# Three rounded score products in place of one full-precision product, the next heads earlier in a pair, and the start and end of a gated mixer in another order

## The reference, cut to what matters

```
# first block, layer l = 0, 1; x is 512 x 1024, ctx is 256 x 1024
h = modulate(rms_norm(x, g_mix[l]), sh1, sc1)          # the same for ctx
f_in, c_q, c_kv, k_rope = split_in_proj(h @ w_in[l])
q = (rms_norm(c_q, g_q) @ w_q_b).reshape(b, n, 12, 96)  # 64 plain + 32 rotated
k, v = from c_kv and k_rope                             # 64 plain + 32 rotated shared
s = einsum(q_nope, k_nope) + einsum(q_rope, k_rope)     # 768 keys
att = softmax(s * 96 ** -0.5) @ v
x = x + gt1 * (concat(fourier_mix(f_in), att) @ w_out[l])
x = x + gt2 * conv_ffn(modulate(rms_norm(x, g_ffn[l]), sh2, sc2))
# layer 0 does the same for ctx, whose 256 queries see the 256 context keys

# second block, the first mixer; hn is the normed output of the first block
proj = hn @ w_in
q, k, v = silu(causal_conv(proj_a)); q, k = l2norm(q), l2norm(k)
oa = rmsnorm(gated_delta_rule(q, k, v, g, beta), norm_a) * silu(z)
ob = rmsnorm(mlstm_chunkwise(qb, kb, vb, i_log, f_log), norm_b) * o_gate
mixed = concat(oa, ob) @ w_out
```

## Time and profile before

| | |
|---|---|
| median of 3 runs | 3251.88 us (3248.88 to 3256.7) |
| the profiled execution | 3250.73 us, span 3248.9 us |
| PE, DVE, ACT, POOL busy | 97%, 48%, 36%, 5% of the span |
| mean granted clock of TensorE | 0.99 |
| attention of layer 0, from the first score to the last | 189.8 to 404.0 us of the span |
| attention of layer 1, likewise | 1181.4 to 1346.0 us |
| gated mixer with its start and end | 1764 to 2215 us |

### The profile page before, as it was taken

One profiled execution on the slowest core, in us unless ns is written; L12 is line 12 of the kernel. 1 busy time (PEld: TensorE's weight loads), 2 busy tenths in 40 slices (PEclk: granted clock), 3 DMA queues, 4 the chain that ended last, 5 costly groups with the idle time before them and its releaser, 6 DMA issues.

```text
span 3248.9 us, 42428 instructions
## 1 busy us (share of the span) xinstructions
PE 3144.0 (97%) x17460; PEld 2482.0 (76%) x17460; DVE 1559.7 (48%) x2346; ACT 1164.4 (36%) x1891; POOL 159.6 (5%) x222
## 2 busy tenths in 40 slices
PE   6999999999999999999999899999999999899999
PEld 4656687887888856788887677887888777788887
DVE  3244545424435445564646554336344577444445
ACT  3134523213223334442434442344222445432233
POOL 0022200000000012100000020000000003000000
PEclk9999999999999999999999999999999999999999
DMA  7500013334112210122232211123232221232222
GB/s 282 220 1 1 1 66 143 116 112 149 66 61 70 84 58 1 40 83 93 98 98 85 75 34 44 42 72 104 85 101 97 69 88 47 72 104 95 93 98 72
DMA packets 74031, 269.28 MB, mean 83 GB/s; under 512 B 9064, under 2 KB 9832, under 8 KB 72560
## 3 DMA queue, kind: packets, MB, share of 16 engines
q1 hardware_dynamic: 73840, 266.57, 23.7%
HBM read 264.44 MB, written 2.10 MB: 82 GB/s over the span
## 4 chain that ended last, share of the span: by engine, by line
PE 92%; DVE 4%; ACT 2%; issue 1%; DMA 1%; SPq 0%; POOL 0%; DVEq 0%; POOLq 0%; ACTq 0%
PE PS L401 68%; PE PS L1383 4%; PE PS L1406 2%; PE PS L1393 2%; PE PS L1309 2%; PE PS L496 1%; DMA room<-in_w_ada 1%; PE PS L1363 1%; PE PS L2983 1%; PE PS L2521 1%; PE PS L580 0%; PE PS L1337 0%; PE PS L1839 0%; PE PS L576 0%; PE PS L2511 0%
## 5 line engine op out<-in xcount | busy, mean ns | idle before, releaser
L401 PE MATMUL PS<-room,WHI 128*128 128x512 f32 (+1 forms) x7200 | 2017.1, 376 | 28.3 <-DVE room L825 6.3
L401 PEld LDWEIGHTS PS<-room,WHI 128*128 128x128 f32 x7200 | 1255.2, 189 | 313.0 <-issue 55.3
L401 PE MATMUL PS<-room,WLO 128*128 128x512 f32 (+1 forms) x3600 | 1234.1, 373 | 0.0
L401 PEld LDWEIGHTS PS<-room,WLO 128*128 128x128 f32 x3600 | 632.5, 188 | 126.5
L340 ACT ACTIVATE WHI<-RING 128x1024 fp32r<-128x1024 f32 x371 | 390.4, 1054 | 570.0 <-PE PS L401 529.1
L349 DVE TENSOR_TENSOR WLO<-RING,WHI 128x1024 fp32r<-128x1024 f32 x371 | 454.4, 1225 | 242.9 <-ACT WHI L340 241.7
L941 DVE SCALAR_TENSOR_TENSOR H<-PS,VEC,H 128x511 f32<-128x511 f32 (+1 forms) x132 | 83.1, 657 | 306.5 <-ACT H L919 306.5
L919 ACT ACTIVATE H<-PS,VEC 128x512 f32<-128x512 f32 (+1 forms) x132 | 88.4, 704 | 347.7 <-PE PS L401 347.7
L1383 PE MATMUL PS<-room 96*128 96x256 f32 (+1 forms) x432 | 155.4, 479 | 10.4 <-DVE room L1545 8.1
L884 DVE SCALAR_TENSOR_TENSOR X<-PS,MOD,X 128x512 f32<-128x512 f32 x96 | 60.5, 658 | 217.4 <-PE PS L401 217.4
L1589 DVE TENSOR_REDUCE room<-PS 128x1 f32<-128x768 f32 (+1 forms) x120 | 101.9, 849 | 100.2 <-PE PS L1383 99.6
(11 more groups left out here) (370 smaller groups left out, 2584.5 us busy)
## 6 DMA issues: line engine op xcount, KB each, us to landing
RING<-in_stream SPq DMA_DIRECT2D x370, 512.0 KB, 3.4
room<-in_w_ada SPq DMA_DIRECT2D x84, 512.0 KB, 5.6
H<-in_w_ada SPq DMA_DIRECT2D x12, 512.0 KB, 4.7
room<-in_consts SPq DMA_DIRECT2D x4, 1024.0 KB, 9.1
room<-in_wq SPq DMA_DIRECT2D x2, 1728.0 KB, 6.8
X<-in_x_in SPq DMA_DIRECT2D x2, 1536.0 KB, 10.0
room<-in_wple SPq DMA_DIRECT2D x2, 1024.0 KB, 4.8
out_dram<-H SPq DMA_DIRECT2D x8, 256.0 KB, 2.1
```

The costliest lines, as they stand in the source:

```text
L401: mm = pe.matmul(acc, wt[:, w], xt[:, k * xw + lo:k * xw + lo + q], start=(k == ks[0] and z == 0), stop=(k == ks[-1] and z == 2))
```

## The change

Two parts. In the attention, Q and K heads are kept as a rounded part (`qh`, `kh`) and a remainder (in the regions of WHI and WLO, since no weights stream there meanwhile), and a score is three products of rounded operands: rounded with rounded, rounded Q with the remainder of K, and the remainder of Q with rounded K. All 128 rows of a head pair are rounded by ACT and their remainder is taken by DVE; the second head's 64 rows, the rotated rows and the key's rotated rows then go to their places by DMAs on SP, from on-chip memory to on-chip memory. The next pair's heads stand in steps 0 to 4 of a pair. "S" and "L" are the rounding and the remainder of the rotated rows and have no product. `in_proj` no longer splits units ahead (`ahead=False`): two of the first three units of the out-projection are split in the last pair and after the last score. The copies of `uv` stand ahead of the rotation of the key.

In the mixer, the two constants and SP's wait move behind the first fetch, the final norm's tiles are written in two groups, three of the gates' ACT functions move one unit later, some products and sums get later ticks, and the rounding of the outputs moves from behind the chains into them, from tick 249 on.

```diff
+    last = pos + (count + WSLOTS if ahead else count)
...
-                split(c, eng, pos + j + 1 + WSLOTS)
+                split(c, eng, min(pos + j + 1 + WSLOTS, last))
...
+HEADS_AT = ((0, "R"), (1, "Q"), (2, "W"), (3, "K"), (3, "S"), (4, "L"))
...
-            for at, kind in ((per - 3, "R"), (per - 3, "Q"), (per - 2, "W"), (per - 2, "K")):
+            for at, kind in HEADS_AT:
                 if i == at and (even or kind in "QK"):
-                    items.append((kind, (p + 1) // 2 if kind in "RW" else p + 1))
+                    items.append((kind, p + 1 if kind in "QK" else (p + 1) // 2))
...
+    first = (0, W, 2 * W)[c.pos % WSLOTS]
+    other = [o for o in (0, W, 2 * W, 3 * W) if not first <= o < first + 2 * W]
+    low_at = ((first, first + W), other)
+
+    def q_at(part, p, z, lo, n, p0, p1):
+        if part:
+            return c.WHI[p0:p1, low_at[p % 2][z] + lo:low_at[p % 2][z] + lo + n]
+        return qh[p0:p1, (2 * (p % 2) + z) * W + lo:(2 * (p % 2) + z) * W + lo + n]
+
+    def k_at(part, p, z, lo, n, p0, p1):
+        if part:
+            return c.WLO[p0:p1, low_at[p % 2][z] + lo:low_at[p % 2][z] + lo + n]
+        return kh[p0:p1, (2 * (p % 2) + z) * W + lo:(2 * (p % 2) + z) * W + lo + n]
...
+        def move_q(p):
+            sp.wait_ge(*q_hi.at(p + 1))
+            sp.dma_start(q_at(0, p, 1, 0, nq, 0, 64).bitcast(F32), q_at(0, p, 0, 0, nq, 64, P).bitcast(F32)).then_inc(*q_moved.up())
+            sp.wait_ge(*q_lo.at(p + 1))
+            sp.dma_start(q_at(1, p, 1, 0, nq, 0, 64).bitcast(F32), q_at(1, p, 0, 0, nq, 64, P).bitcast(F32)).then_inc(*q_moved.up())
...
+        def place_rope(p):
+            sp.wait_ge(*q_moved.at(2 * p + 2))
+            sp.wait_ge(*rope_hi.at(p // 2 + 1))
+            sp.wait_ge(*rope_lo.at(p // 2 + 1))
+            for z in range(2):
+                h = 32 * (2 * (p % 2) + z)
+                for x, rows in ((0, c.RS), (1, c.MS)):
+                    sp.dma_start(q_at(x, p, z, 0, nq, 64, 96).bitcast(F32), rows[h:h + 32, 0:nq]).then_inc(*rope_placed.up())
...
+        def place_key(p):
+            sp.wait_ge(*k_moved.at(2 * p + 2))
+            sp.wait_ge(*key_home.at(4))
+            for x in range(2):
+                sp.dma_start(k_at(x, p, 0, 0, W, 64, 96).bitcast(F32), k_at(x, p, 1, 0, W, 64, 96).bitcast(F32)).then_inc(*key_placed.up())
...
+        for kind, j in items:
+            if kind == "Q":
+                move_q(j)
+                if j % 2:
+                    place_rope(j)
+            elif kind == "L":
+                place_rope(2 * j)
+            elif kind == "K":
+                move_k(j)
+                place_key(j)
...
-            for r, (lo, m) in enumerate(halves(0, n)):
-                mm = pe.matmul(c.bank(b + r, m), q_at(p, z, i * P, P, 0, 96), k_at(p, z, k0 + lo, m, 0, 96), start=True, stop=True)
+                for m in (q_moved, k_moved, key_placed):
+                    pe.wait_ge(*m.at(2 * p + 2))
+                pe.wait_ge(*rope_placed.at(4 * p + 4))
+                if p < 2:
+                    pe.wait_ge(*key_home.at(4))
+            for x, (qx, kx) in enumerate(((0, 0), (0, 1), (1, 0))):
+                for r, (lo, m) in enumerate(halves(0, n)):
+                    mm = pe.matmul(c.bank(b + r, m), q_at(qx, p, z, i * P, P, 0, 96), k_at(kx, p, z, k0 + lo, m, 0, 96),
+                                   start=(x == 0), stop=(x == 2))
...
+            elif kind == "S":
+                act.wait_ge(*rope_sum.at(j + 1))
+                act.activation(c.RS[:, 0:nq].bitcast(F32R), c.MS[:, 0:nq], ACT.Copy).then_inc(*rope_hi.up())
...
+            if j == 5 * per + 1:
+                act.wait_ge(*scores.at(5 * per))
+                split_hi(c, act, c.pos + 1)
+        act.wait_ge(*scores.at(n_steps))
+        split_hi(c, act, c.pos + 2)
...
+            if kind == "Q":
+                dve.wait_ge(*q_hi.at(j + 1))
+                dve.tensor_tensor(q_at(1, j, 0, 0, nq, 0, P), c.PS[:, 512 * b:512 * b + nq],
+                                  q_at(0, j, 0, 0, nq, 0, P).bitcast(F32), ALU.subtract).then_inc(*q_lo.up())
...
+        for t in range(tiles_q):
+            dve.wait_ge(*channels.at(t + 1))
+            dve.tensor_copy(uv(t), c.bank(t)).then_inc(*uv_out.up())
...
-            act.activation(small(0, 1), bias(0), ACT.Exp).then_inc(*g_act.up())
...
+            stream(dve, 0, 3)
...
-        if j == 0:
+        if j == 1:
+            act.activation(small(0, 1), bias(0), ACT.Exp).then_inc(*g_act.up())
...
-            stream(dve)
+            stream(dve, 3, KT)
...
-            yield from until("pe", 48 + 8 * h)
+            yield from until("pe", 48 + 8 * h if h else 51)
...
-            yield from until("pe", 76 + 4 * h)
+            yield from until("pe", 79 + 4 * h)
...
-            yield from until("pe", 121 + 3 * h)
+            yield from until("pe", 121 + 3 * h if h < 3 else 132)
...
+        for i, k in enumerate(OUT_ORDER):
+            yield from until("act", piece_at(i))
+            act.wait_ge(*(fin["a"].at(k + 1) if k < 4 else fin["b"].at(k - 3)))
+            act.activation(oh[:, k * ow:k * ow + NL], mixed(k), ACT.Copy).then_inc(*o_hi.up())
...
-        sp.wait_ge(*made.at(5))
         sp.wait_ge(c.units_done, c.pos)
         lv, causal = CAT["lv0"][0], CAT["causal"][0]
-        sp.dma_start(row4("KEEP"), const(args, "keep", NH2)).then_inc(*loaded.up())
-        sp.dma_start(row4("DROP"), const(args, "drop", NH2)).then_inc(*loaded.up())
...
+    def supply(sp, j):
+        if j == 0:
+            sp.wait_ge(*made.at(5))
+            sp.dma_start(row4("KEEP"), const(args, "keep", NH2)).then_inc(*loaded.up())
+            sp.dma_start(row4("DROP"), const(args, "drop", NH2)).then_inc(*loaded.up())
...
-            for k in order:
-                act.wait_ge(*(fin["a"].at(k + 1) if k < 4 else fin["b"].at(k - 3)))
-                act.activation(xh[:, k * xw:k * xw + NL], source(k), ACT.Copy).then_inc(*hi.up())```

What moves, in rows of the program. First PE in layer 0's first pair, before, at its last four steps (each row of L1383 is a score of 256 keys, L1309 are products for Q and K, L1406 is `values`, L1393 `turn`; a row's bracket names the counters that it waits for):

```order
L1393 MATMUL PS<-ID,SQ 128x128 [waits dve_lane28,act_lane21,pool_lane1]
L1393 MATMUL PS<-ID,SQ 128x128 x5
L1309 MATMUL PS<-room 128x512 [waits act_lane20]
L1309 MATMUL PS<-room 128x512 x2
L1309 MATMUL PS<-room 128x256 x3
L1383 MATMUL PS<-room 128x256 [waits act_lane20]
L1406 MATMUL PS<-room 64x128 [waits dve_lane28,act_lane21]
L1406 MATMUL PS<-room 64x128 x11
L1393 MATMUL PS<-ID,SQ 128x128 [waits dve_lane28,act_lane21,pool_lane1]
L1393 MATMUL PS<-ID,SQ 128x128 x5
L1309 MATMUL PS<-room 128x512 [waits act_lane16,dve_lane22]
L1309 MATMUL PS<-room 128x256
```

More of the change, by code:

```diff
@@ L458, in _ @@
         for j in range(count):
-            fetch(c, sp, args, pos + j + 2 + WSLOTS)
+            fetch(c, sp, args, min(pos + j + 2 + WSLOTS, last + SLOTS))
             if supply is not None:
@@ L1196, in in_proj @@
     linear(c, args, xp, KT, 7, W, ready, lambda j: done.at(j + 1), scalar, None, scalar2, vector2, width=width, fill=fill,
-           supply=supply, slots=2 if l == 0 else MIXED)
+           supply=supply, slots=2 if l == 0 else MIXED, ahead=False)
     if sets:
@@ L1327, in release @@
                 return [probs.at(j + 1)]
-            return [m.at(j + 1) for m in {"R": [r_out], "Q": [q_act, q_dve], "K": [k_act, k_dve], "W": [t_out]}[kind]]
+            if kind in "QK":
+                return [(q_lo if kind == "Q" else k_lo).at(j + 1)]
+            return [(r_out if kind == "R" else t_out).at(j + 1)]
         qnorm.widen(pe)
@@ L1415, in after_score @@
                 turn(a - LAG)
-        for s, (kind, j) in enumerate(items):
+        for s, (kind, j) in enumerate(x for x in items if x[0] not in "SL"):
             b = 2 * (s % 2)
@@ L1426, in _ @@
             after_score(a)
-    slot_of = {item: 2 * (s % 2) for s, item in enumerate(items)}
+    slot_of = {item: 2 * (s % 2) for s, item in enumerate(x for x in items if x[0] not in "SL")}
     slot_of.update({("R", 0): 0, ("Q", 0): 2, ("K", 0): 4, ("W", 0): 6})
@@ L1438, in head @@
         def head(kind, j):
-            b = slot_of[kind, j]
+            b = slot_of.get((kind, j))
             if kind == "R":
@@ L1514, in _, with head @@
             dve.tensor_copy(c.a(vv + t * 768, 768), c.PS[:, 512 * b:512 * b + 768]).then_inc(*v_out_d.up())
+        key, whole = c.a(pr + 6 * W, W, 0, DROPE), c.SQ[0:DROPE, 0:W]
+        def head(kind, j):
+            b = slot_of.get((kind, j))
+            if kind == "Q":
+                dve.wait_ge(*q_hi.at(j + 1))
+                dve.tensor_tensor(q_at(1, j, 0, 0, nq, 0, P), c.PS[:, 512 * b:512 * b + nq],
+                                  q_at(0, j, 0, 0, nq, 0, P).bitcast(F32), ALU.subtract).then_inc(*q_lo.up())
+            elif kind == "K":
+                dve.wait_ge(*k_hi.at(j + 1))
```

(53 more changed lines are left out.)

137 lines of the change are left out of this document (55 added, 82 removed).

## The result

The changed kernel takes 3211.47 us (median of four runs, 3208.14 to 3213.08), the kernel before 3251.27 in the runs beside it: a ratio of 0.9874, 95% interval 0.9857 to 0.9891. It is 39.8 us faster, where 27.5 were forecast. The 3223 us of the forecast were missed by 11.5; the time lies inside the stated range, at the very end of the forecast's own bounds of 3211 to 3235. Its profiled execution spans 3211.2 us, 37.7 less than before.

The account below looks back on a forecast made before the run. PE was taken as the bound. Scores -23, heads +6, short steps +3, splits +4.5, Fourier copies -4 and mixer -14 sum to -27.5, from 3250.7 to 3223 us; own bounds 3211 to 3235, stated range 3200 to 3245.

Parts of the forecast that it names:

- Scores: Attention: 96 scores of 768 keys take 1.06 us instead of 1.30 as three rounded products; -23 us, bounds 15 to 38.
- Heads: Attention: heads between scores cost +17.4 us, less 11.5 for waits and clock drops gone at pairs' starts; net +6.
- short steps: Layer 0's four 256-key steps lose the heads, so small waits come in every pair; +3 us (0 to 6).
- tail: Attention's end: splits behind the last score delay the last copies from banks 4 and 5; +4.5 us (0 to 5).
- 8.1 of waits and the two drops at the pairs' starts: First scores' waits on DVE's last 64-row copy, with clock drops of 1.7 us each, would go; -11.5 us.
- 15.4 for scores behind heads: Attention: 28 heads now between 768-key scores cost PE some 0.55 us each; +15.4 us, bounds 0 and 28.
- signs of being wrong: Listed: scores above 1.14, waits for placed rows, landings over 6 us, new mixer waits of 2 us, attention clock drops.
- Attention in sum: The attention's terms for scores, heads, 256-key steps and the splits at its end, taken together; -9.5 us.
- Fourier copies: Both layers: uv copies ahead of the key's rotation save 2.3 us of two waits and one 1.7 drop; -4 us.
- Mixer: Mixer: 12.7 us of PE waits and two clock drops (3.4) go, 2 us of new waits come; -14 us (-6 to -17).
- DMAs: Head moves: two landings in series of 2.1 us each, hidden behind a pair's steps, so nothing is due.
- rival of slow landings: Layer 1 pairs' first scores wait for landings of 7.3 to 9 us, giving 3241 to 3258; decides from 8.3; chance 0.08.

Follow-up runs that it names:

- one_product: The changed kernel with each score as one float32 product of the rounded parts, remainders made and placed but not multiplied: 3224.48 us, 13.0 above the changed kernel.
- evac_first: The changed kernel with ACT's copy of a turned half ahead of the exponential in steps right behind a head: 3201.06 us, ratio 0.9850.
- old_ticks: The changed kernel with the old ticks of the mixer's pieces: 3220.75 us, the mixer's stage 423.61 us, 15.3 longer.

## Why the prediction was right in sign and 12 us short

- **Scores.** Right: -23 forecast, 22.1 of PE's busy time measured, by the pitch of `linear`'s products. That the score itself is 1.13 and the turn behind it shorter was not foreseen, and cancels. A shorter score uncovers waits beside it, and 7.2 us come back; the forecast counted these at scores behind a head, and not at turns. One reading of the steady stretch before was off, without changing its sum: up to 236.12 it has one turn and the second score, and the second turn stands behind `values`:

```profile
237.59 0.88 PE L1393 MATMUL PS<-ID,SQ 128*128 128x128 f32 x6
```

- **Heads, short steps, tail.** Forecast +6, +3 and +4.5, 13.5 in all. Measured by stages: 7.2 + 2.5 (the rest of the attention part, by `one_product`) = 9.7. The 8.1 of waits and the two drops at the pairs' starts went, as forecast. The mechanism was in part another: scores hardly wait for remainders; turns wait for copies that ACT makes late behind its rounding, and `evac_first` took most of that in layer 0. That these sums came near is luck: of 15.4 for scores behind heads some 7 are found (scores and heads that wait for ACT L1572 or DVE L1604), while the turns' waits for ACT, 7.1 now and 2.7 before, were in no term. The short steps have 11 waits of 0.39, 4.2, where 8 of 2.6 in all stood: +1.6 for a forecast of +3. The tail's wait was there (2.0 in layer 1, 1.3 in layer 0), behind the split that I named; the one in layer 1 brings a clock drop of 3.4 us, one of the signs of being wrong that the forecast had named.
- **Attention in sum.** -9.5 forecast, -12.3 measured.
- **Fourier copies.** -4 forecast, -4.7 in the two stretches ahead of the scores. In layer 0 PE waits 0.83 us ahead of these products, where 1.98 stood; their stretch lost 1.7 with the clock drop.
- **Mixer.** The step that failed in size: -14 forecast, -20.2 measured. The waits were right, 12.7 forecast and 11.9 less idle time in the end. But I gave two clock drops to these waits, at the two that showed next to one. The kernel before has five in the stage, three of them around the later ticks, of which two start 13 us and more behind the last wait. `old_ticks` shows that such drops come with the old ticks: all five together cost 8.3 us of PE's busy time, not 3.4. My two us of new waits were one.
- **DMAs.** No score waits for one, as forecast, but the working was wrong. I counted two landings and gave SP's queue no time; it has three in series before an odd pair (Q's rows, K's, the key's), with 0.5 to 0.6 us for each issue, and before an even pair the rotated rows come last. They land 1.5 to 2.8 us before an odd pair of layer 1, where I had 8, and 0.5 and 0.9 before an even one, where I had 9. The lengths of the pairs were right. The rival of slow landings would have decided at far less than 8.3 us a landing: two more landings in the chain cost 28 us of the 39.8.

Of the 12.3 us, 10.2 show in the profiled spans (37.7 instead of 27.5): 6.2 in the mixer, 2.8 in the attentions, 0.7 ahead of them and 0.5 elsewhere. The rest is the distance of the medians from the spans.

As for the moves themselves, 64 rows of 3 KB landed in 2.5 or 2.6 us and 32 rows of 2 KB in 2.0, so 128 KB more took 0.5 to 0.6, which is 262 to 218 GB/s. The Trainium skill ("SBUF — State Buffer", "Door 1: The DMA port swizzle"), cited in the prediction, gives about 218 GB/s for 64 partitions, half of its figure for all 128. These rows, rounded to 0.1 us, come near that; no run here moved more than 64 rows in this way, so that it is half is not shown.

```profile
WLO<-WLO SPq DMA_DIRECT2D x12, 192.0 KB, 2.6
...
WHI<-WHI SPq DMA_DIRECT2D x6, 192.0 KB, 2.5
...
WHI<-MS SPq DMA_DIRECT2D x12, 64.0 KB, 2.0
```

## What to carry to other kernels

Price a cheaper product by the pitch of the same shape elsewhere in the trace, and then ask which wait it uncovers: of 22 us saved on PE, a third came back. Small transfers that are in order on one queue add up their issues and landings, so walk the queue instruction by instruction; here a place some steps later turned a gain of 40 us into a loss of 47. When a wait goes, look for every clock drop of its stage, not only the one beside it.
